# A norm boundary in a two-block transformer kernel: VectorE writes the first high part of the next input itself

## The reference, cut to what matters

```
def second_block(x, ...):
    for l in range(DEPTH):                                   # DEPTH = 2
        h = rms_norm_2(x, g_pre_mix[l])
        m = hybrid_mixer(h, ...)
        x = x + rms_norm_2(m, g_post_mix[l])
        h = rms_norm_2(x, g_pre_ffn[l])
        f = conv_ffn(h, ...)
        x = x + rms_norm_2(f, g_post_ffn[l])
    return x
```

## Time and profile before

| | before |
|---|---|
| median of 3 runs | 3002.44 us (3001.44 to 3005.16) |
| the profiled execution, its own time | 3000.3 us |
| its span in the profile | 2998.6 us |
| TensorE matmuls busy | 2970.4 us, 99% of the span |
| VectorE busy | 1767.7 us, 59% |
| ScalarE busy | 1266.4 us, 42% |
| GpSimd busy | 151.5 us, 5% |

### The profile page before, as it was taken

How to read it: one execution, slowest core, us unless ns; L and a number is a source line. 1 busy time by engine, 2 the same in 40 slices (tenths; PEclk the granted TensorE clock), 3 DMA queues, 4 the chain that set the end, 5 groups by cost and what they waited for, 6 DMA issues and landing times.

```text
span 2998.6 us, 37756 instructions
## 1 busy us (share of the span) xinstructions
PE 2970.4 (99%) x14612; PEld 2399.2 (80%) x14612; DVE 1767.7 (59%) x3129; ACT 1266.4 (42%) x2377; POOL 151.5 (5%) x203
## 2 busy tenths in 40 slices
PE   9999999999999999999999999999999999999998
PEld 7788888877888888888877688888888776888886
DVE  4666775345555587634465558774355655587743
ACT  4544443322333344432366535443233655354431
POOL 1000000000000000001001101000020011010000
PEclk9999999999999999999999999999999999999999
DMA  4222222222222332234211132222242111233332
GB/s 158 70 100 98 99 99 98 93 77 84 85 77 86 97 99 95 96 98 130 94 36 50 43 99 85 101 96 99 85 125 92 36 43 50 92 92 99 99 98 71
DMA packets 74723, 263.95 MB, mean 88 GB/s; under 512 B 9008, under 2 KB 9008, under 8 KB 74416
## 3 DMA queue, kind: packets, MB, share of 16 engines
q1 hardware_dynamic: 73680, 258.13, 25.9%
q10 hardware_dynamic: 864, 3.41, 0.3%
HBM read 255.74 MB, written 2.10 MB: 86 GB/s over the span
## 4 chain that ended last, share of the span: by engine, by line
PE 89%; DVE 6%; ACT 2%; issue 1%; DMA 1%; POOL 0%; SPq 0%; DVEq 0%; POOLq 0%; ACTq 0%
PE bank L499 24%; PE bank L506 24%; PE bank L502 24%; PE bank L576 2%; PE bank L580 2%; PE bank L577 2%; PE bank L659 2%; PE bank L693 2%; PE bank L674 1%; DVE wl L1440 1%; PE bank L851 1%; PE bank L952 1%; DVE x L1876 1%; DVE big L2036 1%; PE bank L982 1%
## 5 line engine op out<-in xcount | busy, mean ns | idle before, releaser
L1440 DVE TENSOR_TENSOR wl<-ring,wh 128x512 fp32r<-128x512 f32 (+1 forms) x946 | 650.1, 693 | 856.3 <-ACT wh L1038 851.4
L499 PE MATMUL bank<-xh,wh 128*128 128x512 f32 x2464 | 976.0, 396 | 3.4 <-ACT xh L1045 2.7
L502 PE MATMUL bank<-xh,wl 128*128 128x512 f32 x2464 | 961.2, 390 | 2.4 <-DVE wl L1440 2.4
L506 PE MATMUL bank<-xl,wh 128*128 128x512 f32 x2464 | 923.1, 390 | 0.0
L1038 ACT ACTIVATE wh<-ring 128x512 fp32r<-128x512 f32 (+1 forms) x946 | 580.8, 622 | 780.4 <-PE bank L506 699.1
L499 PEld LDWEIGHTS bank<-xh,wh 128*128 128x128 f32 x2464 | 462.9, 188 | 127.1 <-issue 25.5
L506 PEld LDWEIGHTS bank<-xl,wh 128*128 128x128 f32 x2464 | 462.7, 188 | 98.3 <-DVE xl L1545 0.4
L502 PEld LDWEIGHTS bank<-xh,wl 128*128 128x128 f32 x2464 | 463.3, 188 | 94.8 <-DVE wl L1440 4.8
L499 PE MATMUL bank<-bigr,wh 128*128 128x512 f32 x1024 | 399.1, 390 | 0.6 <-ACT bigr L1423 0.6
L502 PE MATMUL bank<-bigr,wl 128*128 128x512 f32 x1024 | 398.6, 389 | 0.0
L506 PE MATMUL bank<-bigr,wh 128*128 128x512 f32 x1024 | 393.6, 389 | 0.0
(11 more groups left out here) (204 smaller groups left out, 2739.7 us busy)
## 6 DMA issues: line engine op xcount, KB each, us to landing
ring<-in_w_up SPq DMA_DIRECT2D x176, 512.0 KB, 3.4
ring<-in_w_down SPq DMA_DIRECT2D x88, 512.0 KB, 3.4
ring<-in_w_in SPq DMA_DIRECT2D x64, 512.0 KB, 3.4
ring<-in_w_ret SPq DMA_DIRECT2D x32, 512.0 KB, 3.2
ring<-in_w_even SPq DMA_DIRECT2D x19, 512.0 KB, 3.2
ring<-in_w_ret_v SPq DMA_DIRECT2D x16, 512.0 KB, 3.2
ring<-in_w_ret_out SPq DMA_DIRECT2D x16, 512.0 KB, 3.2
ring<-in_w_proj SPq DMA_DIRECT2D x16, 512.0 KB, 3.4
```

The source lines that it names most:

```text
L499: e.matmul(o, K.wh(p, c * 128, 128), oh, start=start, stop=False, skip_group_check=True)
L502: e.matmul(o, K.wl(p, c * 128, 128), oh, start=False, stop=False, skip_group_check=True)
L506: m = e.matmul(o, K.wh(p, c * 128, 128), ol, start=False, stop=stop, skip_group_check=True)
L1440: e.tensor_tensor(K.wl(i, 0, w), K.raw(i), K.wh(i, 0, w).bitcast(F32), ALU.subtract).then_inc(F.lo.tell(("piece", i)), 1)
```

## The change

Behind the three boundaries xh(0) of the next input is no longer written by ScalarE from x(0). Since x(0) new = x(0) old + M[0], gain * x(0) new = gain * x(0) old + gain * M[0]. ScalarE writes gain * x(0) old into the temporary tile 3 while the sublayer's last outputs are still being made, and VectorE then writes xh(0) = gain * M[0] + tile 3. M[0] goes into temporary tile 4. VectorE's order at the start becomes m0, xh0, x0, xl0, m1, x1, m2, x2, xl1. The matmuls on `warm` behind the spread are 6 in place of 8. All that waits for xh(0) there now waits for VectorE's semaphore.

```diff
@@ tensor_program
-            q.wait_ge(F.act, ("xh", s, k))
+            q.wait_ge(F.dve if s in POOLED and k == 0 else F.act, ("xh", s, k))
...
         spread(s, 64, 3, F.dve, ("added", s))
         if s != ("p", 1, "f"):
-            keep(8, b)
+            keep(6, b)
@@ scalar_program
-    def post(s, key):
+    def post(s, key, nxt):
...
             if j >= 3:
                 q.wait_ge(F.dve, ("sqa", s, j - 2))
+            if j == 3 and nxt is not None:
+                e.activation(K.tmp(3), K.x(0), ACT.Copy, bias=0.0, scale=K.vec(*GAIN[nxt])).then_inc(
+                    F.act.tell(("xg", nxt)), 1)
             square(s, j, K.bank((*key, j))[:, :])
...
             q.wait_ge(F.dve, ("x", s, j))
-            prescale(s, j)
+            if j:
+                prescale(s, j)
@@ vector_program, post_feed
-            e.scalar_tensor_tensor(out=M[j], in0=M[j], scalar=K.vec(gain, gi + j), in1=BK[3][:, :], op0=ALU.mult,
+            m = M[j] if j else K.tmp(4)
+            e.scalar_tensor_tensor(out=m, in0=M[j], scalar=K.vec(gain, gi + j), in1=BK[3][:, :], op0=ALU.mult,
                                    op1=ALU.mult).then_inc(F.dve.tell(("m", s, j), *([("added", s)] if j == DT - 1 else [])), 1)
             q.wait_ge(F.dve, ("m", s, j))
-            e.tensor_tensor(K.x(j), K.x(j), M[j], ALU.add).then_inc(F.dve.tell(("x", nxt, j)), 1)
-            if j:
+            if j == 0:
+                q.wait_ge(F.act, ("xg", nxt))
+                e.scalar_tensor_tensor(out=K.xh(0), in0=m, scalar=K.vec(*GAIN[nxt]), in1=K.tmp(3), op0=ALU.mult,
+                                       op1=ALU.add).then_inc(F.dve.tell(("xh", nxt, 0)), 1)
+            e.tensor_tensor(K.x(j), K.x(j), m, ALU.add).then_inc(F.dve.tell(("x", nxt, j)), 1)
+            if j == 0:
+                q.wait_ge(F.dve, ("x", nxt, 0))
+                prescale(nxt, 0)
+            if j > 1:
                 prescale(nxt, j - 1)
```

More of the change, by code:

```diff
@@ L1423, in scalar_program @@
             e.activation(K.bigr(m * S), K.GM[m], ACT.Copy, bias=0.0, scale=1.0).then_inc(F.act.tell(("yh", l, m)), 1)
-        post(("p", l, "m"), ("wo", l))
+        post(("p", l, "m"), ("wo", l), ("f", 2 + l))
         ffn(2 + l, True, post_feed(("f", 2 + l)))
-        post(("p", l, "f"), ("down", 2 + l))
+        post(("p", l, "f"), ("down", 2 + l), None if l else ("n", 1))
 def vector_program(e, q, K):
@@ L1446, in prescale @@
     def prescale(s, j):
-        q.wait_ge(F.act, ("xh", s, j))
+        q.wait_ge(F.dve if s in POOLED and j == 0 else F.act, ("xh", s, j))
         e.scalar_tensor_tensor(out=K.xl(j), in0=K.x(j), scalar=K.vec(GAIN[s][0], GAIN[s][1] + j),
```

## The result

The changed kernel took 3007.63 us (median of 22 runs, 3005.34 to 3011.84), the kernel before 3002.57 us in the 22 runs beside it (3000.84 to 3008.49). The ratio is 1.0015, with a 95% interval of 1.0009 to 1.0021: by the ratio slower by 4.5 us, between 2.7 and 6.3 (the two medians lie 5.1 apart).

The account below looks back on a forecast made before the run. TensorE's work bounds the kernel, but VectorE's list ends each boundary's group. Each boundary loses 1.59 us (0.67 the added instruction, the rest GpSimd's adds), three 4.8: 3002.44 + 4.8 = 3007.2 us, range 3005.5 to 3009.0.

Parts of the forecast that it names:

- What bounds the stretch: Behind each boundary, VectorE's whole list sets the group's end; TensorE's start, 0.71 us sooner, only lengthens its wait for wl8.
- The added instruction: VectorE's xh0 behind m0 at each boundary, taken like an xl: 0.67 us to the next instruction, 0.75 to its end.
- The copies on ScalarE: Three gained copies of x(0), 0.72 us each, in ScalarE's 2.03 us pause before its square: cost nothing; uncovered, at most 2.2.
- The walk: Step-by-step times of VectorE, GpSimd and TensorE at the first boundary with the change: 1.59 us lost per boundary.
- that tie: VectorE's xl1 against GpSimd's add1 behind x2: xl1 starts 0.06 us ahead, so it was taken to go first.
- the rival in which GpSimd goes first there: At xl1, add1 runs first and the old pattern follows 0.78 us late: 2.3 us in all, 3004.8; chance 0.15.
- The new one at k = 2: New TensorE stop at the third tile of k = 2, waiting for wl3: 1.85 us.
- the one at wl8: TensorE's stop within the group for the low part of weights wl8, four tiles after the new stop: 1.2 us.
- The waits of L502: TensorE's waits for low parts of weights (wl): about 8 to 9 us in total in place of 2.4.
- The clock did not fall in the new stop: Rival: TensorE's clock falls in the 1.85 us stop, 5.0 us more at one boundary, 3012.2 (all three 3022); chance 0.11.
- the earlier start is kept: Rival: VectorE's list also ends 0.71 us sooner at each boundary, gaining 2.1 us in all, 3000.3; chance 0.07.
- nothing comes of it: Rival: xh0 is held back, TensorE starts as before and the lists shift by little: 3002.4; chance 0.07.

Follow-up runs that it names:

- e2: Changed kernel with xl0 put back behind x1, xh0 still written by VectorE: 3005.53 us, against 3002.72 for the kernel before beside it.
- e4: Kernel before with one more VectorE instruction of the added kind, between m0 and x0, writing an unused tile: 3005.03 us, against 3002.72 for before.
- e1: Changed kernel with 8 matmuls on the constant tile behind the spread in place of 6: 3008.23 us, against 3002.72 for the kernel before.
- e3: Kernel before with only VectorE's order changed, xl0 right behind x0, nothing added: 3010.46 us, against 3002.72 for the kernel before.
- e5: Kernel before with six of GpSimd's seven adds of squares left out at each boundary, for timing alone: 3000.67 us, against 3002.86 for before.
- e6: Changed kernel with six of GpSimd's seven adds of squares left out at each boundary, for timing alone: 3000.03 us, against 3002.86 for before.
- e7: Kernel before with VectorE writing wl8 ahead of m7 and x7 in place of behind xl7: 3001.20 us, against 3002.86 for the kernel before.
- e9: Changed kernel with xl0 back behind x1, wl8 ahead of m7, wl3 ahead of the output norm's mean: 2999.97 us, against 3003.69 for before.
- e8: Changed kernel with xl0 back behind x1, wl8 ahead of m7, wl3 in the pause before the spread: 3000.82 us, against 3002.86 for before.
- e10: Changed kernel with xl0 back behind x1 and wl8 ahead of m7, wl3 where it was: 3001.39 us, against 3003.69 for before.

## Why the prediction was right

**What bounds the stretch.** The statement that the group's end is set by VectorE's list and not by TensorE's start is shown by e2 and e4 against each other (TensorE's start 1.36 us apart, L 0.02 apart) and by both against the kernel before (one instruction more on VectorE, L up by 0.65 and 0.67 us). e4 alone would not show it, since there TensorE's start is late by 0.67 us as well, and e1, built for this question, did not move the start.

**The added instruction.** Taken like an xl, 0.75 us to its end and 0.67 to the next; measured 0.75 and 0.67.

**The copies on ScalarE.** They cost nothing, as forecast, but not because ScalarE's pause covers them. The copy stands behind the wait for the output tile, not in the 2.03 us ahead of it, as ScalarE's timeline in the kernel after shows:

```profile
1772.66 0.73 ACT L1321 ACTIVATE tmp<-x,vec 128x512 f32<-128x512 f32 x1 [2.03 <-PE bank L506]
1773.29 0.58 ACT L1049 ACTIVATE tmp<-bank 128x512 f32<-128x512 f32 x1
```

So this square begins 0.63 us later than it would. The next ones come at their old times (1778.10, before 1778.16), and m0 with them: nothing waited for the late one. Here the reason was wrong and the price right.

**The order of the collisions.** The walk had xl1 ahead of add1 by 0.06 us; it was 0.05. It had add2 ahead of xl2 and add3 ahead of wl3; both came. wl3 was to end 11.47 us after m0 and ended at 11.43 (1809.69 less 1798.26). That this pattern is what costs the rest was shown from both sides: e3 makes it with nothing added, e2 takes it away and leaves the addition. e5 and e6 show that GpSimd's adds are its cause: without them the change gains. The one place where I had to choose was that tie, and the rows say more on it than the prediction took from them. It gave the turn to GpSimd whenever VectorE's instruction ends and GpSimd waits. But add1 before had begun 0.61 us ahead of xl1, and add7 0.11 ahead of wl8: in each case the one that began first in the trace went first. Counted over the twelve profiled kernels, an add and an instruction of VectorE with two operands in SBUF overlap in 345 places, and in 344 the one that began first also ended first; in the last (e4, third boundary) they began 3 ns apart. By that order xl1, begun 0.05 us ahead, had to win, so the rival in which GpSimd goes first there hung only on whether the start times of the walk were right to 0.06 us. They were, and with terms rounded to 0.01 us over several steps that was in part luck. I did not build a kernel for that rival.

**The stops.** The new one at k = 2 was forecast with 1.85 us and is in the profile with 1.54, the one at wl8 with 1.2 and 0.93. Half of each difference comes from comparing two different things: the idle time in brackets counts from the modelled end of the last matmul, 0.39 us after its start, while my lengths counted from its successor's due start, 0.23 us after. With these 0.16 us added the stops are 1.70 and 1.09, still 0.15 and 0.11 short. Most of the rest is that behind a stop the next matmul begins 0.34 us later (1809.75 to 1810.09) and not 0.23, 0.11 us that the walk left out twice: behind the stop for wl3, and at a small stop that it did not have. x1 now comes later, so TensorE's first matmul of k = 1 has to wait for xh(1), which shows on its weight load alone:

```profile
1803.38 0.19 PEld L499 LDWEIGHTS bank<-xh,wh 128*128 128x128 f32 x1 [0.28 <-ACT xh L1045]
```

The moments at which TensorE went on were right: 26.38 us after m0 forecast for wl8, 26.32 measured. The waits of L502 were forecast with 8 to 9 us, although the walk's own stops come to about 9.6 with the 0.5 elsewhere; 7.8 were measured, and the same two causes make up the difference.

**The sum.** 1.59 us per boundary were forecast and 1.53 measured by L; 4.8 and 4.6 us in all, within the 2.7 to 6.3 of the timed runs. That the forecast time, 3007.2 us, lies 0.4 from the measured median says less than it seems, since that interval is 3.6 us wide; L is what confirms the size. The span was forecast at 3003.4 and came at 3006.1; L gives 3003.2, and the other 2.9 us are the clock's between the second and the third boundary, which I took as fixed.

**The rivals.** The clock did not fall in the new stop. Here are two windows of the kernel after, the first with the stop in it and the second behind it; the granted clock stands third from the end, 1.00 in both:

```profile
1808.00:1812.00 4.00, 2.46 (x11) 1.87 (x11) 3.96 (x6) 0.40 (x2) 1.14 (x1) 1.00 0.30 93
1812.00:1816.00 4.00, 4.00 (x19) 3.31 (x18) 3.97 (x6) 2.57 (x5) 1.29 (x1) 1.00 0.50 171
```

That the earlier start is kept was ruled out by the stops in the profile, and e6 shows what it would have taken. That nothing comes of it was ruled out as well: xh(0) was not held back, VectorE wrote it at 1799.04 right behind m0. I had noted wl8's stop as the bound but not asked whether it could be moved; e7 shows that it was worth more (0.96 us per boundary) than all of the change's purpose.

## What to carry to other kernels

When an engine starts sooner, look for its next stop before counting the gain: here the second wait of the same group took it back. And before an experiment that moves a start is believed, look in its trace whether the start moved (e1). Two engines that can't run certain instructions at once have an order between them that is set by hundredths of a microsecond, and putting one instruction elsewhere, with no work added, cost 1.7 us, 0.9 of them a wait at its new place and 0.8 the collisions behind it; so after any move, walk both timelines together from the first point that shifts, with GpSimd's instructions in it. The best place for a piece of work that others wait for was a pause in which neither of the two engines had anything else (e9), and the best repair was the piece that came last in the list and was needed first (e7).

## What was not expected of the hardware

The granted clock was the largest thing left out of the sum. Behind the second boundary TensorE waits about 3.45 us for a rotated input in both kernels, and the clock falls. In the kernel after (the third number from the end of a window is the granted clock):

```profile
2222.29 13.86 PE L901 MATMUL bank<-big,ring 64*64 64x32 f32 x256 [3.47 <-DVE tmp L1494]
```

```profile
2219.00:2222.00 3.00, 0.00 (x0) 0.00 (x0) 1.74 (x3) 0.00 (x0) 1.67 (x1) 0.86 0.82 265
...
2235.00:2240.00 5.00, 5.00 (x39) 4.93 (x38) 1.39 (x8) 1.31 (x4) 1.37 (x1) 0.50 0.41 104
```

In the kernel before:

```profile
2216.00:2219.00 3.00, 0.00 (x0) 0.00 (x0) 1.74 (x3) 0.00 (x0) 1.63 (x1) 1.00 0.73 235
...
2235.00:2240.00 5.00, 5.00 (x42) 4.67 (x40) 1.93 (x3) 1.26 (x4) 1.73 (x2) 1.00 0.79 264
```

The same matmuls took 12.64 us before. After, the clock fell within TensorE's pause itself (0.86 in that window), 1.1 us before its end, and was still at half, 1.2 GHz, up to 2240. Before, it was at 1.00 in the pause from 2216 to 2219, fell only when the matmuls ran again, and was at full again from 2235 on. The pauses were equally long, 3.45 and 3.47 us.

By the clock records in the traces the stretch at half lasted 13.7 us before and 20.5 after. Without the 1.1 us in the pause that is 5.7 us more of work at half speed, and half of it, 2.9 us, is what the way from the second boundary's sum of squares to the third boundary's m0 took longer: 422.5 against 419.6. The other runs fall in line, there and ahead of the first boundary:

| stretch | at half clock | its time | runs |
|---|---|---|---|
| second boundary's sum to third's m0 | 13.7 us | 419.6, 419.7 us | before, e9 |
| | 17.1 us | 421.2 to 421.6 us | e1, e2, e4, e5, e7, e8, e10 |
| | 20.5 us | 422.1 to 422.5 us | after, e3, e6 |
| start to the first boundary's m0 | 3.4 us | 1798.3 to 1799.1 us | before, after, e2, e4, e8, e9 |
| | 6.8 us | 1799.7 to 1800.6 us | e1, e6, e7, e10 |
| | 10.2 us | 1801.8, 1802.1 us | e5, e3 |

The change has no instruction in the stretch between the boundaries, and adds none to TensorE ahead of the first. So the clock makes single executions differ by 3 us behind one pause and by nearly 4 ahead of the first boundary, as much as this change moved. What sets how long it stays down was not tested, nor whether the change has a part in it, since each kernel has one profile.

The other thing was the root in e8: a GpSimd instruction of 128x4 elements, 1.01 us alone, was held up for 0.37 us by a VectorE instruction with two operands in SBUF. The Trainium skill, page "SBUF — State Buffer", section "Who interferes with whom", calls the pair of ports that the two engines share an exclusive lock, and says, of VectorE's two-port modes, that whoever issues first has it for the whole instruction. It names no least size. Here wl3, which is no such mode but has two operands in SBUF, was first (1796.43 against 1796.60), and the trace agrees with 1.38 in place of 1.01 us.
